# ScalarE's order in the scan loop, the scores around the scan input, and Gelu ahead of the last attention head

## The chip, the cores and the metric

The kernel runs on one core of a Trainium2 chip. The metric is the device time of one execution in microseconds, as the median over several runs. A core has TensorE (PE in the profile, with its weight loads as PEld), VectorE (DVE), ScalarE (ACT), GpSimd (POOL) and SyncE (SP, which issues most of the DMA transfers here). Each engine works through its own list of instructions in order, and waits on semaphores for what the others produce.

## The reference

Two layers over 256 tokens of width 1024. Each layer computes, in float32:

```
proj  = rms_norm(x) @ w_in            # q, k, v, u and two gate vectors
a     = differential attention: softmax(q0 k0) - lam * softmax(q1 k1), times v, 4 heads,
        then rms_norm per head
s     = bidirectional diagonal state-space scan of u (16 pairs of groups, both directions)
s     = gelu(s);  s = s * sigmoid(s @ w_glu)
x     = x + (g0 * (a @ w_branch0) + g1 * (s @ w_branch1)) @ w_out
x     = x + SwiGLU (layer 0)   or   top-2-of-8 expert SwiGLU (layer 1)
```

The change lies in the middle of the first five lines, once in each layer.

## The kernel before

Weights stream through SBUF in tiles of 128x2048 (1 MB). A tile is loaded into `raw` by SP, rounded by ScalarE into `hi` (`split` on ScalarE, L1016), and VectorE subtracts to get `lo` (`split` on VectorE, L1362). TensorE multiplies each tile as hi*hi, hi*lo and lo*hi, 24 matmuls of 512 columns (`proj`, printed as L549, since one helper issues nearly all matmuls). The tiles of a mixer are numbered from `t`; `t+8` to `t+15` belong to the gates, `t+16` is the second factor of the scan branch (`w_glu`), `t+17` to `t+20` the two branch matrices, `t+21` to `t+24` `w_out`.

The scan loop (`for s in range(8)`) handles in each turn three things at once: one of 8 attention blocks (head `s//2`, half of the tokens `s%2`), one of 8 pieces of the state-space scan, and one gate tile. What each engine does in turn `s`, in the order in which its code is written:

- TensorE: input of scan piece s+1 (`s5_in`, 32 small matmuls), the two halves of the scores of block s (`scores`, the second half waits for the first), transposes of the weights of block s-1 (`weights_t`, L704), the gate tile `t+8+s`, the attention output of block s-1 (`head_out`), and the scan output of piece s (`s5_out`). In the last turn `s5_out(7)` stands ahead of the gate tile.
- VectorE: `lo` of tile `t+10+s`, row minimum of block s (L1456), scan piece s+1 (`s5_scan`, L1429 to L1437), the softmax factors of block s (L1460, L1461), the combined weights of block s (L1468).
- ScalarE: tables for piece s+1 (`scan_tables`, L1121, L1127), `hi` of tile `t+10+s`, two exponentials of block s (L1071); in odd turns the evacuation of two gate banks through Tanh (`from_pj`, L1065); then `head_back` of block s-1, that is the copy of its transposed weights (L1083) for which `head_out` waits, and, once `head_out` is done, a copy (L1088) and a Square with a sum (L1089); and last the scaled second half of the softmax of block s (`scale_second`, L1077), for which VectorE's L1468 waits.
- GpSimd: the elementwise phase turns before and after each scan piece (`turn_forward`, L1893 to L1900); `s5_out` waits for them.

The scores of block s use the PSUM bank that VectorE's L1468 of block s-1 has read last, so `scores(s)` waits for it.

After the loop TensorE still has block 7: transposes, `head_out(7)`, then `channels`, 32 matmuls that regroup the scan's output after Gelu. ScalarE finishes block 7, takes the Sqrt for the heads' norm (L1194), runs Gelu (L1197), copies the regrouped scan output (L1200, `at_hi`), and VectorE makes its `lo` (L1558); then `proj(t+16)` can start. Between the halves of that projection TensorE transposes the attention output (`attention_t`, L567); after it, it transposes the scan output for the element-wise product (L567), and `proj(t+17)` follows, which needs the evacuation of `t+16` through Tanh (L1065 again) and both parts of the attention transposes (L1028 and L1376).

ScalarE evaluates functions from tables; `ACT_TABLE_LOAD` in the trace is a change of the loaded set.

Of the kernel before, what the change touches and what calls it, by code (L numbers as in the profile page):

```python
# [101 lines left out]
def build(nc, x, norm_mix, w_in, attn_lambda, attn_subln, ssm_lam_re, ssm_lam_im, ssm_log_dt, ssm_b_re, ssm_b_im,  # L102
# [6 lines left out]
    with ctx:  # L109
# [149 lines left out]
        def col(i, n=1):  # L259
            return small[:, i:i + n]  # L260
# [37 lines left out]
        def at_count(l, kind, g):  # L298
            return l * AT_PER_LAYER + AT_ORDER[(kind, g)] + 1
# [247 lines left out]
        def _(pe):  # L547
# [166 lines left out]
            def mixer(l):  # L714
# [54 lines left out]
                for s in range(8):  # L769
                    if s < 7:  # L770
                        s5_in(l, s + 1)
                    scores(l, s, 0)
                    scores(l, s, 1)
                    if s > 0:
                        weights_t(l, s - 1)
                    if s == 7:
                        s5_out(l, 7)
                    proj(t + 8 + s, l, 4 + s // 2, 4 * (s % 2), s % 2 == 0, s % 2 == 1)
                    if s == 0:
                        pe.wait_ge(pj_free[1], pj_read(l, 3))  # L780
                    if s > 0:
                        head_out(l, s - 1)
                    if s < 7:
                        s5_out(l, s)
                weights_t(l, 7)
                head_out(l, 7)
                channels(l)
# [12 lines left out]
                proj(t + 16, l, 8, 4, True, True, attention_t)  # L800
                pe.wait_ge(at_lo_ready, at_count(l, "a", 1))
                pe.wait_ge(s_ready, 2 * l + 2)
                for th in range(TH):
                    transposes((l, "s", th), [s_t[:, k, th * P:(th + 1) * P] for k in range(4)])
                proj(t + 17, l, 9, 0, True, True)
# [203 lines left out]
        def _(act):  # L1009
# [68 lines left out]

            def head_back(l, j):
                name = (l, "o", j)  # L1080
                bank = TR[TURN[name] % 2]
                act.wait_ge(wt_tr, 8 * l + j + 1)
                act.activation(wdiff_t, bank[:, 0:2 * P].rearrange("p (t q) -> p t q", t=2), ACT.Copy).then_inc(wt_ready, 1)  # L1083
                wait_turn(act, name)
# [45 lines left out]
            def mixer(l):  # L1130
# [48 lines left out]
                for s in range(8):  # L1179
# [3 lines left out]
                    probs_of(l, s)  # L1183
                    if s % 2 == 1:
                        i = 4 + s // 2
                        g, n = (i - 4) // 2, (i - 4) % 2
                        from_pj(l, i, t + 8 + s, lambda th: gates[:, th, g, n * 512:(n + 1) * 512], ACT.Tanh,
                                lambda th: col(RH + th))
                    if s > 0:
                        head_back(l, s - 1)  # L1190
                    scale_second(l, s)
                head_back(l, 7)
                act.wait_ge(avar_ready, l + 1)
                act.activation(col(AR, 8), col(AV, 8), ACT.Sqrt).then_inc(aroot_ready, 1)  # L1194
                act.wait_ge(y_done, DUOS * (l + 1))
                for half in range(2):
                    act.activation(s4[:, 512 * half:512 * half + 512], PY[half][:, :], ACT.Gelu).then_inc(gelu_ready, 1)  # L1197
                for th in range(TH):
                    act.wait_ge(chan_full, 2 * l + th + 1)
                    act.activation(at_hi[:, 4:8, th * P:(th + 1) * P], PV[th][:, :].rearrange("p (k s) -> p k s", k=4),  # L1200
                                   ACT.Copy).then_inc(at_hi_ready, 1)
                for th in range(TH):
# [153 lines left out]
        def _(dve):  # L1356
# [139 lines left out]
            def mixer(l):  # L1496
# [46 lines left out]

                wait_read(dve, (l, "o", 6))
# [4 lines left out]
                for th in range(TH):  # L1549
# [4 lines left out]
                    if th == 0:  # L1554
                        for h in range(TH):
                            half = slice(h * P, (h + 1) * P)
                            dve.wait_ge(at_hi_ready, at_count(l, "sa", h))
                            tt(at_lo[:, 4:8, half], PV[h][:, :].rearrange("p (k s) -> p k s", k=4),  # L1558
                               at_hi[:, 4:8, half].bitcast(f32), SUB).then_inc(at_lo_ready, 1)
# [418 lines left out]
```

## Time and profile before

| what | value |
|---|---|
| median of 3 runs | 1546.03 us (1545.55 to 1546.53) |
| the profiled execution | 1545.13 us, of which the span of the trace is 1543.3 us |
| busy: PE, PEld, DVE, ACT, POOL | 92%, 76%, 74%, 58%, 20% of the span |
| scan loop of layer 0 | about 129 to 209 us, its tail until 224 us |
| scan loop of layer 1 | about 558 to 639 us, its tail until 653 us |
| everything after the mixers | SwiGLU of layer 0 from 298 us, experts from 720 us |

The busy share of an engine says how much of the span it worked, not what bounds the end; for that the waits and the chain of work are read. All times in the rows below are microseconds from the start of the span.

### The profile page before, as it was taken

How to read it: one execution, taken by the hardware profiler on the slowest of the kernel's cores; microseconds unless marked ns; L12 is line 12 of the kernel's file. 1: busy time of each engine (PE TensorE's matmuls, PEld its weight loads, DVE VectorE, ACT ScalarE, POOL GpSimd, SP SyncE). 2: the span in 40 equal slices, each digit the busy share in tenths (PEclk: the TensorE clock that was granted, in tenths of full speed). 3: DMA queues.
4: the chain of work that ended last, by engine and by line, in shares of the span. 5: the costliest groups of instructions: out<-in, count | busy, mean ns of one | idle time of the engine just before them, and what ended most of it. 6: DMA issues, size and time to landing. Idle time of an engine off the chain costs nothing.

```text
span 1543.3 us, 24088 instructions
## 1 busy us (share of the span) xinstructions
PE 1423.8 (92%) x8701; PEld 1165.2 (76%) x8701; DVE 1146.9 (74%) x1125; ACT 894.3 (58%) x986; POOL 309.6 (20%) x354
## 2 busy tenths in 40 slices
PE   5688969999998989698999999999999999999995
PEld 3476748788887777487788888888878888888884
DVE  6966637655446556376888889888898899888985
ACT  4234544544335355444776777777677677676774
POOL 3747741998000067100000000000000000000000
PEclk9899979999999999898999999999999999999998
DMA  9332234555554423194999999999999999999970
GB/s 267 103 103 86 95 95 162 180 169 191 193 183 145 157 71 109 54 337 156 321 369 340 350 344 341 359 331 353 365 317 360 336 350 363 323 359 321 359 268 27
DMA packets 273808, 374.64 MB, mean 243 GB/s; under 512 B 17616, under 2 KB 220752, under 8 KB 273616
## 3 DMA queue, kind: packets, MB, share of 16 engines
q1 hardware_dynamic: 270176, 367.51, 70.8%
q0 software_dynamic: 1280, 3.15, 1.1%
q10 hardware_dynamic: 2288, 3.11, 0.6%
q8 instruction: 42, 0.69, 0.2%
q14 instruction: 22, 0.18, 0.0%
HBM read 371.63 MB, written 1.05 MB: 241 GB/s over the span
## 4 chain that ended last, share of the span: by engine, by line
PE 77%; DVE 8%; ACT 5%; issue 5%; DMA 1%; SPq 1%; POOL 1%; DVEq 0%; ACTq 0%; POOLq 0%
PE bank L549 75%; ACT hi L1016 3%; DVE lo L1362 3%; PE bank L946 1%; SPq L424 1%; PE bank L567 1%; DVE at_lo L1778 1%; DMA raw<-in_w_out_dram 1%; DMA areg<-in_norm_mix_dram 1%; DVE at_lo L1748 1%; DVE at_lo L1376 0%; PE bank L860 0%; PE bank L704 0%; POOL raw L1893 0%; ACT raw L1104 0%
## 5 line engine op out<-in xcount | busy, mean ns | idle before, releaser
L1362 DVE TENSOR_TENSOR lo<-raw,hi 128x2048 fp32r<-128x2048 f32 x347 | 805.2, 2325 | 191.4 <-ACT hi L1016 182.2
L1016 ACT ACTIVATE hi<-raw 128x2048 fp32r<-128x2048 f32 x347 | 662.9, 1914 | 115.0 <-PE bank L549 112.9
L549 PE MATMUL bank<-hi,at_hi 128*128 128x512 f32 x1280 | 518.3, 405 | 35.4 <-DVE areg L1414 13.7
L549 PE MATMUL bank<-hi,at_lo 128*128 128x512 f32 x1280 | 503.6, 393 | 0.0
L549 PE MATMUL bank<-lo,at_hi 128*128 128x512 f32 x1280 | 503.4, 393 | 0.0
L549 PEld LDWEIGHTS bank<-hi,at_hi 128*128 128x128 f32 x1280 | 242.9, 190 | 89.7 <-issue 17.3
L549 PEld LDWEIGHTS bank<-hi,at_lo 128*128 128x128 f32 x1280 | 242.8, 190 | 52.2
L549 PEld LDWEIGHTS bank<-lo,at_hi 128*128 128x128 f32 x1280 | 243.7, 190 | 46.1
L549 PE MATMUL bank<-hi,ht_hi 128*128 128x512 f32 x440 | 172.2, 391 | 4.4 <-DVE ht_lo L1679 3.5
L549 PE MATMUL bank<-hi,ht_lo 128*128 128x512 f32 x440 | 171.3, 389 | 0.0
L549 PE MATMUL bank<-lo,ht_hi 128*128 128x512 f32 x440 | 171.3, 389 | 0.0
L1272 ACT ACTIVATE ht_hi<-bank 128x256 fp32r<-128x256 f32 (+1 forms) x99 | 40.5, 409 | 167.2 <-PE bank L946 122.3
L549 PEld LDWEIGHTS bank<-hi,ht_hi 128*128 128x128 f32 x440 | 82.6, 188 | 24.7 <-DVE ht_lo L1679 6.1
L549 PEld LDWEIGHTS bank<-hi,ht_lo 128*128 128x128 f32 x440 | 82.6, 188 | 17.3
L549 PEld LDWEIGHTS bank<-lo,ht_hi 128*128 128x128 f32 x440 | 82.6, 188 | 16.9
L1893 POOL TENSOR_TENSOR raw<-raw 128x256 f32<-128x256 f32 x64 | 48.4, 787 | 217.8 <-issue 188.1
L1679 DVE TENSOR_TENSOR ht_lo<-bank,ht_hi 128x256 fp32r<-128x256 f32 (+1 forms) x99 | 44.3, 448 | 42.4 <-ACT ht_hi L1272 42.4
L549 PE MATMUL bank<-raw 64*64 64x64 f32 (+1 forms) x1664 | 51.8, 235 | 14.7 <-issue 8.6
L1310 ACT ACTIVATE vreg<-bank 128x256 f32<-128x256 f32 x88 | 33.8, 384 | 53.0 <-PE bank L549 53.0
L549 PEld LDWEIGHTS bank<-raw 64*64 64x64 f32 (+1 forms) x1664 | 48.3, 135 | 18.4 <-issue 9.8
L549 PE MATMUL bank<-vreg,qk 128*128 128x128 f32 x320 | 42.4, 285 | 10.8 <-ACT qk L1083 9.4
L549 PEld LDWEIGHTS bank<-vreg,qk 128*128 128x128 f32 x320 | 40.2, 198 | 15.8 <-ACT qk L1083 13.2
(265 smaller groups left out, 1096.5 us busy)
## 6 DMA issues: line engine op xcount, KB each, us to landing
raw<-in_moe_w_dram SPq DMA_DIRECT2D x528, 512.0 KB, 5.5
raw<-in_ffn_w_dram SPq DMA_DIRECT2D x66, 512.0 KB, 4.2
raw<-in_w_in_dram SPq DMA_DIRECT2D x64, 512.0 KB, 4.6
raw<-in_w_branch_dram SPq DMA_DIRECT2D x16, 512.0 KB, 4.1
raw<-in_w_out_dram SPq DMA_DIRECT2D x16, 512.0 KB, 4.9
raw<-in_w_glu_dram SPq DMA_DIRECT2D x4, 512.0 KB, 4.2
xres<-in_x_dram SPq DMA_DIRECT2D x2, 512.0 KB, 6.1
areg<-in_norm_mix_dram ACTq DMA_DIRECT2D x2, 512.0 KB, 6.4
```

The source lines that it names most:

```text
L424: sp.dma_start(dst, src).then_inc(raw_full[slot], 16)
L549: return pe.matmul(o, a, b, start=start, stop=stop)
L567: last = pe.transpose(bank[:, i * rows:(i + 1) * rows], src, ident[0:rows, 0:rows])
L946: m = pe.transpose(TR[0][:, f * P:(f + 1) * P], v_flat[:, FC + f * P:FC + (f + 1) * P], ident)
L1016: act.activation(hi[:, slot, :], src, ACT.Copy).then_inc(hi_ready, 1)
L1272: act.activation(ht_hi[:, :, 0:cols], TR[0][:, 0:2 * cols].rearrange("p (f s) -> p f s", f=2), ACT.Copy).then_inc(ht_hi_ready, 1)
L1310: act.activation(v_flat[:, 0:FC], h_bank(c)[:, 0:FC], ACT.Silu).then_inc(g_ready, 1)
L1362: tt(lo[:, slot, :], src, hi[:, slot, :].bitcast(f32), SUB).then_inc(lo_ready, 1)
L1679: tt(ht_lo[:, :, 0:cols], TR[0][:, 0:2 * cols].rearrange("p (f s) -> p f s", f=2), ht_hi[:, :, 0:cols].bitcast(f32), SUB).then_inc(ht_lo_r ...
L1748: tt(at_lo[:, 4 * g:4 * g + 4, 0:P], banks[4 + g][:, :].rearrange("p (k c) -> p k c", k=4), at_hi[:, 4 * g:4 * g + 4, 0:P].bitcast(f32), S ...
L1778: m = stt(at_lo[:, 4 * n:4 * n + 4, P:2 * P], PY[n][:, :].rearrange("p (k c) -> p k c", k=4), place_gate, at_hi[:, 4 * n:4 * n + 4, P:2 * ...
L1893: last = tt(dst, src[:, :, :, d, :], w[:, r:r + 1, :, d, :].broadcast_to([P, 2, 2, 64]), MUL)
```

## The change

On ScalarE the copy of the transposed weights is taken out of `head_back` (`weights_back`) and stands right behind the exponentials, `scale_second` follows it, then come the gates of the odd turns, then the rest of `head_back`. In the last turn Gelu stands between `scale_second` and the gates. After the loop the copies of the regrouped scan output stand ahead of the rest of block 7 and of the Sqrt.

On TensorE the first half of the scores stands ahead of `s5_in`, `channels` ahead of `head_out(7)`, and the attention transposes stand behind `proj(t+16)` instead of between its halves. VectorE makes the `lo` of the regrouped scan output ahead of the heads' norm.

```diff
                 for s in range(8):
+                    scores(l, s, 0)
                     if s < 7:
                         s5_in(l, s + 1)
-                    scores(l, s, 0)
                     scores(l, s, 1)
...
                 weights_t(l, 7)
+                channels(l)
                 head_out(l, 7)
-                channels(l)
                 pe.wait_ge(at_lo_ready, at_count(l, "sa", 1))
...
-                proj(t + 16, l, 8, 4, True, True, attention_t)
+                proj(t + 16, l, 8, 4, True, True)
+                attention_t()
+                pe.wait_ge(s_ready, 2 * l + 2)
+                for th in range(TH):
+                    transposes((l, "s", th), [s_t[:, k, th * P:(th + 1) * P] for k in range(4)])
                 pe.wait_ge(at_lo_ready, at_count(l, "a", 1))
-                pe.wait_ge(s_ready, 2 * l + 2)
-                for th in range(TH):
-                    transposes((l, "s", th), [s_t[:, k, th * P:(th + 1) * P] for k in range(4)])
                 proj(t + 17, l, 9, 0, True, True)
...
+            def weights_back(l, j):
+
+                act.wait_ge(wt_tr, 8 * l + j + 1)
+                act.activation(wdiff_t, TR[TURN[(l, "o", j)] % 2][:, 0:2 * P].rearrange("p (t q) -> p t q", t=2),
+                               ACT.Copy).then_inc(wt_ready, 1)
...
                     probs_of(l, s)
+                    if s > 0:
+                        weights_back(l, s - 1)
+                    scale_second(l, s)
+                    if s == 7:
+                        act.wait_ge(y_done, DUOS * (l + 1))
+                        for half in range(2):
+                            act.activation(s4[:, 512 * half:512 * half + 512], PY[half][:, :], ACT.Gelu).then_inc(gelu_ready, 1)
...
                     if s > 0:
                         head_back(l, s - 1)
-                    scale_second(l, s)
+                weights_back(l, 7)
+                for th in range(TH):
+                    act.wait_ge(chan_full, 2 * l + th + 1)
+                    act.activation(at_hi[:, 4:8, th * P:(th + 1) * P], PV[th][:, :].rearrange("p (k s) -> p k s", k=4),
+                                   ACT.Copy).then_inc(at_hi_ready, 1)
                 head_back(l, 7)
```

What the instruction lists show. In the first place, an odd turn of the loop on ScalarE (turn 1 of layer 0), bank6 holds the scores, bank7 the transposed weights and the attention output, bank0 and bank1 the gate tiles. Before:

```order
L1071 ACTIVATE bank6,small<-bank6,small 128x256
L1065 ACTIVATE gates<-bank0,small 128x512 [waits pj0_full]
L1065 ACTIVATE gates<-bank1,small 128x512 [waits tile_used]
L1083 ACTIVATE qk<-bank7 128x256 [waits wt_tr]
L1088 ACTIVATE areg<-bank7 128x128 [waits cbm_in,tr_full]
L1089 ACTIVATE bank7,small<-bank7 128x128 [waits act_own]
L1077 ACTIVATE qk<-bank6,small 128x256 [waits factor_ready]
L1121 ACTIVATE raw<-par 128x4x63 [waits zs_ready]
L1127 ACTIVATE raw<-raw 128x4x32 [waits wtab_half]
L1127 ACTIVATE raw<-raw 128x4x32
L1016 ACTIVATE hi<-raw 128x2048 [waits tile_used,raw_full0]
```

The same turn with the change (its line numbers stand 1 to 8 higher):

```order
L1072 ACTIVATE bank6,small<-bank6,small 128x256
L1083 ACTIVATE qk<-bank7 128x256 [waits wt_tr]
L1078 ACTIVATE qk<-bank6,small 128x256 [waits factor_ready]
L1066 ACTIVATE gates<-bank0,small 128x512 [waits pj0_full]
L1066 ACTIVATE gates<-bank1,small 128x512 [waits tile_used]
L1092 ACTIVATE areg<-bank7 128x128 [waits cbm_in,tr_full]
L1093 ACTIVATE bank7,small<-bank7 128x128 [waits act_own]
L1125 ACTIVATE raw<-par 128x4x63 [waits zs_ready]
L1131 ACTIVATE raw<-raw 128x4x32 [waits wtab_half]
L1131 ACTIVATE raw<-raw 128x4x32
L1017 ACTIVATE hi<-raw 128x2048 [waits tile_used,raw_full0]
```

The gates and the two instructions of `head_back` stood ahead of the scaled second half (L1077) and now stand between it (L1078) and the next tile's `hi` (L1017).

In the second place, ScalarE after the loop in layer 0. Before:

```order
L1194 ACT_TABLE_LOAD
L1194 ACTIVATE small<-small 128x8 [waits avar_ready]
L1197 ACT_TABLE_LOAD
L1197 ACTIVATE raw<-bank 128x512 [waits y_done]
L1197 ACTIVATE raw<-bank 128x512
L1200 ACTIVATE at_hi<-bank 128x4x128 [waits chan_full] x2
L1204 ACTIVATE ureg<-bank 128x4x128 [waits at_lo_ready] x2
L1016 ACTIVATE hi<-raw 128x2048 [waits tile_used,raw_full0]
L1028 ACTIVATE at_hi<-bank 128x4x128 [waits tr_full] x2
L1050 DMA areg<-in_norm_ffn_dram 128x1024
L1065 ACTIVATE qk<-bank 128x512 [waits pj0_full]
L1065 ACTIVATE qk<-bank 128x512 [waits tile_used]
```

With the change, from the copies of the regrouped scan output on (Gelu and its table load stand in the last turn of the loop now):

```order
L1205 ACTIVATE at_hi<-bank 128x4x128 [waits chan_full] x2
L1092 ACTIVATE areg<-bank 128x128 [waits tr_full]
L1093 ACTIVATE bank,small<-bank 128x128 [waits act_own]
L1209 ACT_TABLE_LOAD
L1209 ACTIVATE small<-small 128x8 [waits avar_ready]
L1212 ACTIVATE ureg<-bank 128x4x128 [waits at_lo_ready] x2
L1017 ACTIVATE hi<-raw 128x2048 [waits tile_used,raw_full0]
L1029 ACTIVATE at_hi<-bank 128x4x128 [waits tr_full] x2
L1051 DMA areg<-in_norm_ffn_dram 128x1024
L1066 ACT_TABLE_LOAD
L1066 ACTIVATE qk<-bank 128x512 [waits pj0_full]
L1066 ACTIVATE qk<-bank 128x512 [waits tile_used]
```

The Sqrt is now behind Gelu, and a third table load per layer stands ahead of the Tanh that evacuates tile `t+16`.

In the third place, TensorE after the last gate tile of layer 0. L704 are the transposes of block 7, `qk` with `vreg` is `head_out`, `raw` with `cst` is `channels`. Before:

```order
L549 MATMUL bank<-vreg,qk 128x128 [waits wt_ready]
L549 MATMUL bank<-vreg,qk 128x128
L704 MATMUL bank<-cst,qk 128x128 [waits w_ready]
L704 MATMUL bank<-cst,qk 128x128
L549 MATMUL bank<-vreg,qk 128x128 [waits wt_ready]
L549 MATMUL bank<-vreg,qk 128x128
L549 MATMUL bank<-raw,cst 32x4x64 [waits gelu_ready]
L549 MATMUL bank<-raw,cst 32x4x64 x15
L549 MATMUL bank<-hi,at_hi 128x512 [waits pj_free0,lo_ready,at_lo_ready]
```

With the change:

```order
L549 MATMUL bank<-vreg,qk 128x128 [waits wt_ready]
L549 MATMUL bank<-vreg,qk 128x128
L704 MATMUL bank<-cst,qk 128x128 [waits w_ready]
L704 MATMUL bank<-cst,qk 128x128
L549 MATMUL bank<-raw,cst 32x4x64 [waits gelu_ready]
L549 MATMUL bank<-raw,cst 32x4x64 x15
L549 MATMUL bank<-vreg,qk 128x128 [waits wt_ready]
L549 MATMUL bank<-vreg,qk 128x128
L549 MATMUL bank<-hi,at_hi 128x512 [waits pj_free0,lo_ready,at_lo_ready]
```

`head_out(7)` moved from before `channels` to behind it.

## Rows read from the trace of the kernel before

**Rows 1.** Grouped waits of TensorE, 133 to 228 us: total us, times, longest.

```profile
PE bank L549 <- ACT qk L1083: 4.7, 5, 1.1
```

**Rows 2.** Timeline of ScalarE, loop of layer 0: start, length, what, [idle before, releaser].

```profile
153.63 1.91 ACT L1016 ACTIVATE hi<-raw 128x2048 fp32r<-128x2048 f32 x1
...
161.46 0.69 ACT L1065 ACTIVATE gates<-bank,small 128x512 f32<-128x512 f32 x1 [1.14 <-PE bank L549]
162.05 0.38 ACT L1083 ACTIVATE qk<-bank 128x256 f32<-128x256 f32 x1
163.23 0.28 ACT L1088 ACTIVATE areg<-bank 128x128 f32<-128x128 f32 x1 [0.80 <-PE bank L549]
...
163.80 0.47 ACT L1077 ACTIVATE qk<-bank,small 128x256 f32<-128x256 f32 x1
164.16 0.41 ACT L1121 ACTIVATE raw<-par 128x252 f32<-128x252 f32 x1
...
164.86 1.90 ACT L1016 ACTIVATE hi<-raw 128x2048 fp32r<-128x2048 f32 x1
...
186.01 1.90 ACT L1016 ACTIVATE hi<-raw 128x2048 fp32r<-128x2048 f32 x1
```

**Rows 3.** Timeline of VectorE, loop of layer 0: three factor instructions and one split.

```profile
140.85 0.16 DVE L1461 TENSOR_TENSOR small<-small 128x1 f32<-128x1 f32 x1
...
162.33 0.16 DVE L1461 TENSOR_TENSOR small<-small 128x1 f32<-128x1 f32 x1
...
173.42 0.16 DVE L1461 TENSOR_TENSOR small<-small 128x1 f32<-128x1 f32 x1
...
197.14 2.32 DVE L1362 TENSOR_TENSOR lo<-raw,hi 128x2048 fp32r<-128x2048 f32 x1 [1.31 <-ACT hi L1016]
```

**Rows 4.** Timeline of GpSimd, the last two instructions of the last scan piece.

```profile
197.39 2.65 POOL L1899 TENSOR_TENSOR raw<-raw 128x256 f32<-128x256 f32 x1
200.00 0.72 POOL L1900 TENSOR_TENSOR raw<-raw 128x256 f32<-128x256 f32 x1
```

**Rows 5.** Chain of work that ended last, 183 to 234 us: start, length, what.

```profile
200.77 8.51 PE bank L549 x64
...
212.77 0.43 PE bank L704 x2
...
213.66 0.73 PE bank L549 x4
...
215.10 1.28 ACT L1194
...
224.13 4.78 PE bank L549 x12
...
229.78 2.75 PE bank L549 x12
```

**Rows 6.** Timeline of ScalarE, the second copy of the attention transposes, layer 0.

```profile
229.88 0.59 ACT L1028 ACTIVATE at_hi<-bank 128x512 fp32r<-128x512 f32 x1
```

**Rows 7.** Timeline of TensorE, first matmul of projection t+17, layer 0.

```profile
233.17 0.48 PE L549 MATMUL bank<-hi,at_hi 128*128 128x512 f32 x1
```

**Rows 8.** Chain of work, layer 1: the gates behind the last gate tile.

```profile
638.76 0.69 ACT gates L1065
```

**Rows 9.** Timeline of TensorE, layer 1: channels, first matmuls of t+16 and t+17.

```profile
648.50 3.23 PE L549 MATMUL bank<-raw,cst 128*32 128x256 f32 x32 [4.68 <-ACT raw L1197]
...
653.19 0.50 PE L549 MATMUL bank<-hi,at_hi 128*128 128x512 f32 x1 [1.45 <-DVE at_lo L1558]
...
660.47 0.48 PE L549 MATMUL bank<-hi,at_hi 128*128 128x512 f32 x1
```

**Rows 10.** Timeline of VectorE, layer 1: `lo` of tile t+18.

```profile
655.60 2.29 DVE L1362 TENSOR_TENSOR lo<-raw,hi 128x2048 fp32r<-128x2048 f32 x1 [1.42 <-ACT hi L1016]
```

**Rows 11.** Busy time by window: us, PE, PEld, DVE, ACT, POOL, granted clock, DMA, GB/s.

```profile
141.00:162.00 21.00, 19.98 (x212) 15.86 (x212) 13.91 (x21) 10.73 (x29) 17.05 (x24) 1.00 0.30 94
...
200.00:210.00 10.00, 8.49 (x64) 6.98 (x64) 0.38 (x3) 2.41 (x7) 7.24 (x11) 0.83 0.54 146
```

More of the change, by code:

```diff
@@ L799, in gated_s_t @@
                         transposes((l, "s2", th), heads_of(s_gated, th))
-                proj(t + 16, l, 8, 4, True, True, attention_t)
-                pe.wait_ge(at_lo_ready, at_count(l, "a", 1))
+                proj(t + 16, l, 8, 4, True, True)
+                attention_t()
                 pe.wait_ge(s_ready, 2 * l + 2)
@@ L804, in mixer @@
                     transposes((l, "s", th), [s_t[:, k, th * P:(th + 1) * P] for k in range(4)])
+                pe.wait_ge(at_lo_ready, at_count(l, "a", 1))
                 proj(t + 17, l, 9, 0, True, True)
@@ L1077, in scale_second @@
                 act.activation(second, TR[TURN[(l, "sc", j)] % 2][:, SEQ:2 * SEQ], ACT.Copy, scale=col(C1)).then_inc(second_scaled, 1)
+            def weights_back(l, j):
+                act.wait_ge(wt_tr, 8 * l + j + 1)
+                act.activation(wdiff_t, TR[TURN[(l, "o", j)] % 2][:, 0:2 * P].rearrange("p (t q) -> p t q", t=2),
+                               ACT.Copy).then_inc(wt_ready, 1)
             def head_back(l, j):
                 name = (l, "o", j)
[L1081 to L1084, printed above, removed]
+                bank = wait_turn(act, name)
                 h, th = j // 2, j % 2
@@ L1190, in mixer @@
                         head_back(l, s - 1)
-                    scale_second(l, s)
[L1192 to L1197, printed above, removed]
+                weights_back(l, 7)
                 for th in range(TH):
@@ L1201, in mixer @@
                                    ACT.Copy).then_inc(at_hi_ready, 1)
+                head_back(l, 7)
+                act.wait_ge(avar_ready, l + 1)
+                act.activation(col(AR, 8), col(AV, 8), ACT.Sqrt).then_inc(aroot_ready, 1)
                 for th in range(TH):
@@ L1542, in mixer @@
                     weights(l, s)
+                for h in range(TH):
+                    half = slice(h * P, (h + 1) * P)
+                    dve.wait_ge(at_hi_ready, at_count(l, "sa", h))
+                    tt(at_lo[:, 4:8, half], PV[h][:, :].rearrange("p (k s) -> p k s", k=4),
+                       at_hi[:, 4:8, half].bitcast(f32), SUB).then_inc(at_lo_ready, 1)
                 wait_read(dve, (l, "o", 6))
@@ L1553, in mixer @@
                     m.then_inc(a_ready, 1)
[L1554 to L1559, printed above, removed]
                 split_static(t + 18)
```

## The prediction

> **What bounds the kernel now.** I read four views, in this order. The grouped waits of TensorE show who stops it in the loop: in layer 0 it waits five times, 4.7 us in all, for the copy of the transposed weights (L1083) [rows 1], which stands on ScalarE behind the second gate bank and so behind the end of the gate tile. Between these waits TensorE is busy (19.98 of 21.00 us in the window of turns 1 to 3) and the clock is at 2.4 GHz [rows 11]. The loop is TensorE's, then, but the timelines of ScalarE and VectorE show a second loop close behind, and it is the one the change touches. The chain of waits shows the tail: from the end of the last gate tile (200.77 + 8.51 = 209.28) to the first matmul of `t+16` (224.13) it takes 14.85 us, through six hand-overs and two table loads of 1.28 us in a row [rows 5], with TensorE all but idle. Layer 1 repeats this: 638.76 to 653.19, 14.43 us [rows 8, 9]. What comes after is a steady stream on TensorE, so I take a shift there one to one into the end.
>
> **The second loop.** VectorE makes `lo`, the row minimum, the next scan piece and the factors in one go; it starts when ScalarE's `hi` is there. From the start of `hi` to the end of the factors: 153.63 to 162.49, and 164.86 to 173.58, 8.86 and 8.72 us, mean 8.79 [rows 2, 3]. Then ScalarE runs `scale_second`, 163.80 to 164.16 (0.36), the tables, 164.16 to 164.86 (0.70), and the next `hi` [rows 2]. Before the change nothing else stands between factors and `hi`, if the rest was done under the scan.
>
> **What the loop costs after the change.** The rest of `head_back`, 163.23 to 163.80 (0.57), and in odd turns the two Tanh, 2 x 0.59 = 1.18 (161.46 to 162.05 is one pitch), now stand between factors and the next `hi` [rows 2]. With 0.04 for a hand-over (POOL's end 200.72 to TensorE's 200.77 [rows 4, 5]) an even turn's tail is 0.04 + 0.36 + 0.57 + 0.70 = 1.67 and an odd one's 2.85. Two turns take 2 x 8.79 + 4.52 = 22.10 us; before they took 164.86 to 186.01, 21.15 [rows 2]. So the order that frees TensorE from its wait of up to 1.1 in each odd turn [rows 1] makes ScalarE and VectorE the bound, 0.95 slower per pair. From the first factors (141.01 [rows 3]), which nothing moves, to the `hi` of turn 6 there are three odd and two even tails and four stretches: 141.01 + 8.55 + 3.34 + 35.16 = 188.06 instead of 186.01, **+2.05**. The scan piece of turn 6 and GpSimd's states for `s5_out(7)`, for which TensorE waits at 200.77, are late by that. Scores ahead of `s5_in` hide the first half's drain, but TensorE, with 21.15 - 1.1 = 20.05 us of work in 22.10, waits for `weights` anyway: counted at nothing. If this cover were gone, it would gain at most a few tenths per turn.
>
> The bounds of this term: GpSimd's L1899 began 0.25 after VectorE's split and took 2.65, until 0.6 behind the split's end (199.46), where its neighbour L1900 took 0.72 [rows 3, 4]. Which of the two meets the split depends on the phase. If it is L1900 alone, the states come with the split's end and one instruction behind it, 199.46 + 0.7 and so 0.6 less late; if both are held, one instruction more, +0.6.
>
> **The tail.** Scaling, weights and Gelu of the last turn now run under the last gate tile: Gelu needs `s5_out(7)`, which ends where the 5.5 us of the gate tile begin, then 1.28 for its table and, as an estimate from the two 512-column Tanh, 1.2 for itself: it is done 3 us before the gate tile. What is left behind the gate tile on TensorE is `head_out(6)` 0.73 (as the one at 213.66), the transposes of block 7 0.43 [rows 5], `channels` 3.23, and from its end (651.73) to `t+16` (653.19) 1.46 for `at_hi` and `at_lo` [rows 9]. `head_out(7)` fits into these 1.46. Sum 5.85. So `t+16` starts at 209.28 + 2.05 + 5.85 = 217.18 in layer 0, 6.95 earlier, and at 638.76 + 2.05 + 5.85 = 646.66 in layer 1, 6.53 earlier.
>
> **From t+16 to t+17.** Before this took 233.17 - 224.13 = 9.04 in layer 0, where the first half ran at a low clock (4.78 for 12 matmuls against 2.75 [rows 5]), and 7.28 in layer 1 [rows 7, 9]. After: 24 matmuls, 2 x 2.75 and 0.1 for filling, 5.6. The attention transposes follow, and their second copy starts 0.97 behind the matmuls (228.91 to 229.88 [rows 5, 6]), at 6.6; the next ScalarE instruction comes 0.5 later, and it is now a table load, 1.28 (as the Sqrt's at 215.10), then Tanh 0.6: 9.0 us after the start the bank is free and `t+17` can begin. The other path into `t+17` is shorter: `hi` of `t+18` behind Sqrt and two copies, its `lo` 2.29 [rows 10] done at about 6.85, then two `at_lo` of 0.65, 8.15. What the halves of `t+16` used to hide, the trip of the attention transposes over ScalarE and VectorE, is thus open now, 9.0 - 5.6 - 1.7 for both sets of transposes, 1.7 us. Layer 0: 217.18 + 9.0 = 226.2 against 233.17, **-7.0**. Layer 1: 655.7 against 660.47, -4.8. In layer 1 the `w_out` loads, queued among expert tiles, are let go by `lo` of `t+18`: before 657.89 - 653.19 = 4.7 after the start of `t+16`, now 6.85, so this stream moves by 6.53 - 2.15 = 4.4 only [rows 9, 10]. I take **-4.6** between the two.
>
> At the table load the Trainium skill speaks against the change. The row has the load at 1.28 us and the chain has nothing behind it: the Sqrt's load begins where block 7's Square ends [rows 5]. "ScalarE: Activation LUTs", section "What ACT_TABLE_LOAD costs", gives 1.283 us for the load and 1.38 us more for a drain at each change of set; by that the estimate would be 1.4 us more per layer, -8.8 in all. By the row it is -11.6.
>
> **Sum.** -7.0 - 4.6 = -11.6. The profiled execution took 1545.13 (span 1543.3 and 1.8 around it), so 1533.5; the median of before is 0.9 higher, **1534.4 us**. A measurement of this kernel tells about 0.2%, 3.1 us, from no change.
>
> **Rivals.**
> - *The loop loses nothing.* If the second loop has slack that I don't see, both +2.05 fall away: -15.7, 1530.3. For it: TensorE did set the pace before. Against: every stretch of 8.79 is serial on two in-order engines. Chance 0.13.
> - *The table load costs twice.* A pause as long as the load itself, behind the third load of each layer, delays `t+17` by 1.3 each: 1537.0. For it: the load stands alone on the way to `t+17`. Against: no such pause in the chain. The skill's drain, above, would be this case. Chance 0.11.
> - *Layer 1's gain is held by its loads.* If the 10 MB of `w_out` and expert tiles arrive when they did before, the 4.6 are lost: 1539.0. For it: the stream of loads is dense there. Against: its trigger moves by 4.4. Chance 0.12.
> - *Slower: the clock.* TensorE's idle time per pair of turns grows from 1.1 to over 2. In the window behind the wait for `s5_out(7)` the granted share was 0.83; in the loop with its waits of 1.1 it was 1.00 [rows 1, 11]. If the longer gaps bring 1.2 GHz into the loop, a gate tile takes 4.78 x 2 instead of 5.5, some 4 us more, and a turn then is TensorE's at about 14 us instead of 11: 3 us in each of 12 turns, 36 us, 1570. It decides from the fourth such turn on. "TensorE: Matmul & The Clock Gate", section "HAM oscillation — how this bites in real kernels", has such an oscillation from regular waits in a loop; the window of the loop with waits of 1.1 does not show it. Against: the gaps stay under 2 us. Chance 0.05.
> - *It gives nothing to speak of*, a new wait in the tail that eats most of it, as Gelu late for `channels`: it would have to come some 14 us later than I sum in the two layers together, since it has 4 us of cover in each (3 and the 1.16 ahead of `channels`). Near 1546. Chance 0.04.
>
> My case has 0.55. Its own range is 1532 to 1537 (GpSimd's collision, -0.6 to +0.6 per layer, and either path into `t+17`, 8.15 or 9.0). The range for 8 in 10 takes in the loop without loss and the held loads: 1529.5 to 1539.5. Faster by over 0.2%: my case, the first three rivals, less a little for two of them together with a slower loop, 0.89; within 0.2%: 0.05; slower 0.06.
>
> **What the profile after would show.** In odd turns no wait of TensorE for the weights' copy; instead a wait for VectorE's combined weights ahead of `scores(s)` of about 0.8 and 1.9 us in alternating turns. `hi` tiles 22.1 us apart per pair, and the wait ahead of `s5_out(7)` ending at 202.8. No table load between the end of the last gate tile and `t+16`, and 5.9 us between them. A table load and about 1.7 us of idle TensorE ahead of `t+17`. `t+16` at 217.2, and in layer 1 at 639.7 (646.66 less the 7.0 of layer 0). Wrong would be: a `hi` pace of 21.1 or less (first rival), a granted clock below 1 in the loop (the fourth), ScalarE idle for loads in layer 1 between `t+20` and `t+24` (the third).

## The result and the profile after

The changed kernel takes 1534.28 us (median of 4 runs, 1533.64 to 1534.79), the one before 1545.79 us beside it (4 runs, 1545.37 to 1546.53): a ratio of 0.9925, 95% interval 0.9908 to 0.9942. The profiled execution took 1534.32 us with a span of 1532.5. The forecast was 1534.4.

The sum came out, but several of its terms did not; they cancel in part. So the stages are read one at a time. First the grouped waits of TensorE of the changed kernel, 133 to 228 us, where [rows 1] had the copy of the transposed weights:

```profile
PE bank L549 <- DVE qk L1476: 4.3, 4, 1.5
PE bank L549 <- POOL raw L1907: 3.3, 1, 3.3
PE bank L567 <- DVE at_lo L1384: 1.1, 1, 1.1
PE bank L549 <- DVE at_lo L1555: 0.8, 1, 0.8
```

The waits for the copy are gone. Of the 4.7 us in [rows 1] three waits of 1.05 us lay in the loop; the other two stood in its tail (TensorE before):

```profile
210.32 0.71 PE L549 MATMUL bank<-vreg,qk 128*128 128x128 f32 x4 [1.05 <-ACT qk L1083]
...
213.66 0.71 PE L549 MATMUL bank<-vreg,qk 128*128 128x128 f32 x4 [0.47 <-ACT qk L1083]
```

In place of the 3.1 us in the loop TensorE now waits 4.3 us there for the combined weights (L1476) ahead of the scores: the loop's wait has moved and grown, it has not gone.

Timeline of ScalarE in the loop of layer 0, which answers to [rows 2]:

```profile
142.69 0.47 ACT L1078 ACTIVATE qk<-bank,small 128x256 f32<-128x256 f32 x1 [2.52 <-DVE small L1469]
143.06 0.68 ACT L1066 ACTIVATE gates<-bank,small 128x512 f32<-128x512 f32 x1
145.32 0.69 ACT L1066 ACTIVATE gates<-bank,small 128x512 f32<-128x512 f32 x1 [1.57 <-PE bank L549]
...
147.17 1.90 ACT L1017 ACTIVATE hi<-raw 128x2048 fp32r<-128x2048 f32 x1
...
169.36 1.90 ACT L1017 ACTIVATE hi<-raw 128x2048 fp32r<-128x2048 f32 x1
...
191.55 1.90 ACT L1017 ACTIVATE hi<-raw 128x2048 fp32r<-128x2048 f32 x1
```

The `hi` tiles are 22.19 us apart per pair of turns (169.36 to 191.55) where they were 21.15 [rows 2]. The first odd turn shows something more: between the two Tanh ScalarE waits 1.57 us for TensorE's gate tile, and the next `hi` stands behind that wait, as it did in the old order.

VectorE and GpSimd at the end of the loop, as in [rows 3, 4]:

```profile
142.50 0.16 DVE L1469 TENSOR_TENSOR small<-small 128x1 f32<-128x1 f32 x1
...
203.10 2.70 DVE L1370 TENSOR_TENSOR lo<-raw,hi 128x2048 fp32r<-128x2048 f32 x1 [1.88 <-ACT hi L1017]
```

```profile
202.94 0.72 POOL L1906 TENSOR_TENSOR raw<-raw 128x256 f32<-128x256 f32 x1
203.62 2.77 POOL L1907 TENSOR_TENSOR raw<-raw 128x256 f32<-128x256 f32 x1
```

One of GpSimd's two last instructions is held again while VectorE's split runs, the other of them than before; from the start of the first to the end of the second it is 3.4 us before (197.39 to 200.72) and 3.5 now. The first factors meant in the prediction, those of turn 1, end at 142.66 here and at 141.01 before. This 1.65 us does not come from the moved instructions: the `hi` of turn 0 already starts at 120.51 instead of 118.85, and the distance stays the same up to here. The point differs from run to run (138.12 to 142.66 over all kernels below), so I count the stages from it.

TensorE from the last scan output on, answering to [rows 5, 7, 9]:

```profile
201.28 1.45 PE L549 MATMUL bank<-qk,ureg 64*128 64x256 f32 x4 [1.45 <-DVE qk L1476]
...
206.44 2.40 PE L549 MATMUL bank<-raw 64*64 64x64 f32 x40 [3.29 <-POOL raw L1907]
...
214.77 0.60 PE L549 MATMUL bank<-vreg,qk 128*128 128x128 f32 x4
215.21 0.38 PE L704 MATMUL bank<-cst,qk 128*128 128x128 f32 x2
215.53 1.93 PE L549 MATMUL bank<-raw,cst 128*32 128x256 f32 x32
...
218.90 0.50 PE L549 MATMUL bank<-hi,at_hi 128*128 128x512 f32 x1 [0.80 <-DVE at_lo L1555]
...
224.48 1.04 PE L567 MATMUL bank<-cst,areg 128*128 128x128 f32 x8
226.59 1.16 PE L567 MATMUL bank<-cst,ureg 128*128 128x128 f32 x8 [1.07 <-DVE at_lo L1384]
228.26 0.47 PE L549 MATMUL bank<-hi,at_hi 128*128 128x512 f32 x1 [0.51 <-ACT qk L1066]
```

No table load lies on the way from the gate tile (its end is 206.44 + 8.51 = 214.95, the same 8.51 as in [rows 5]) to `t+16` (the Sqrt's starts at 218.83, when `t+16` is ready), and the way is 3.95 us instead of 14.85. `channels` take 1.93 us; they took 3.23 in [rows 9].

Against the point where the first factors end, in layer 0:

| from the first factors to | before | after | difference |
|---|---|---|---|
| `hi` of turn 6 | 45.00 | 48.89 | +3.89 |
| `s5_out(7)` | 59.76 | 63.78 | +4.02 |
| `t+16` | 83.12 | 76.24 | -6.88 |
| `t+17` | 92.16 | 85.60 | -6.56 |

Layer 1 from `t+17` of layer 0 to its own: 427.30 before [rows 7, 9]; after, by TensorE's timeline there:

```profile
637.21 1.93 PE L549 MATMUL bank<-raw,cst 128*32 128x256 f32 x32
...
640.58 0.50 PE L549 MATMUL bank<-hi,at_hi 128*128 128x512 f32 x1 [0.80 <-DVE at_lo L1555]
...
649.95 0.47 PE L549 MATMUL bank<-hi,at_hi 128*128 128x512 f32 x1 [0.51 <-ACT qk L1066]
```

649.95 - 228.26 = 421.69, so -5.61. From there to the end the span changes by -0.28 (882.83 to 882.55). With the +1.65 ahead of the factors: 1.65 - 6.56 - 5.61 - 0.28 = -10.8, the difference of the two spans.

### The profile page after: what moved, and what is told of

Same layout as the page of the kernel before. It is cut to its first block, busy times and chain, and to the rows that moved or that the text cites. A ratio compares the mean times of both kernels' runs of the same rounds, so it can differ in the third digit from the quotient of the medians.

```text
span 1532.5 us, 24090 instructions
## 1 busy us (share of the span) xinstructions
PE 1423.9 (93%) x8701; PEld 1166.7 (76%) x8701; DVE 1148.6 (75%) x1125; ACT 896.0 (58%) x988; POOL 309.7 (20%) x354
## 3 DMA queue, kind: packets, MB, share of 16 engines
HBM read 371.63 MB, written 1.05 MB: 243 GB/s over the span
## 4 chain that ended last, share of the span: by engine, by line
PE 72%; DVE 11%; ACT 7%; issue 6%; DMA 1%; SPq 1%; POOL 1%; ACTq 0%; DVEq 0%; POOLq 0%
PE bank L549 70%; ACT hi L1017 4%; DVE lo L1370 3%; SPq L424 1%; PE bank L947 1%; DVE raw L1445 1%; PE bank L567 1%; DVE at_lo L1785 1%; DMA areg<-in_norm_mix_dram 1%; DMA raw<-in_w_out_dram 1%; DVE at_lo L1755 1%; DVE bank L1438 0%; DVE small L1464 0%; DVE raw L1437 0%; POOL raw L1907 0%
## 5 line engine op out<-in xcount | busy, mean ns | idle before, releaser
L1017 ACT ACTIVATE hi<-raw 128x2048 fp32r<-128x2048 f32 x347 | 663.0, 1914 | 116.2 <-PE bank L549 113.5
L1072 ACT ACTIVATE bank<-bank,small 128x256 f32<-128x256 f32 x32 | 14.2, 443 | 53.0 <-DVE small L1464 53.0
```

The source lines that it names most:

```text
L1017: act.activation(hi[:, slot, :], src, ACT.Copy).then_inc(hi_ready, 1)
```

## The experiments

Eleven runs of eight kernels in three groups, each group beside runs of the kernel before; the first group ran on one chip, the other two on another. Times compare directly only inside a group.

### First group: the parts of the loop

`e1_noswap`: the change without its first edit on TensorE.

```diff
-                    scores(l, s, 0)
                     if s < 7:
                         s5_in(l, s + 1)
+                    scores(l, s, 0)
                     scores(l, s, 1)
```

> The changed kernel with one part undone: the scan input (32 small matmuls) stands ahead of both score halves again. Theory S: the alternation of scores and scan input keeps TensorE's clock at 1.2 GHz for longer behind the first stall of the loop (granted 0.50 from 133 to 139 us, where the kernel before had 0.97), so without it turn 1 comes about 1.7 us earlier in each layer: 1531, about 3 us less than the changed kernel's 1534.3. Rival: the low clock has another cause, and the order of scores is worth nothing either way: 1534.3 within 0.5.

`e2_scale_last`: that, and in turns 0 to 6 the scaled second half last, with the copy of the weights still first.

```diff
                     if s > 0:
                         weights_back(l, s - 1)
-                    scale_second(l, s)
                     if s == 7:
+                        scale_second(l, s)
...
                     if s > 0:
                         head_back(l, s - 1)
+                    if s < 7:
+                        scale_second(l, s)
```

> As the run without the alternation, and in turns 0 to 6 the scaled second half stands last on ScalarE again, behind gates and the rest of block s-1; only the copy of the transposed weights stays ahead of the gates; turn 7 and the tail as changed. Theory M (the serial loop of ScalarE and VectorE sets the pace after the change, because gates and the rest of block s-1 stand between the factors and the next tile's hi): the hi tiles come 20.1 us apart per pair instead of 22.2, the last scan piece about 7 us earlier in each layer, 1520. Rival F (that loop is free and TensorE sets the pace): at most 1 us less than the run without the alternation.

`e3_old_loop`: `e1_noswap` with turns 0 to 6 of ScalarE wholly in the old order (gates, copy, rest of `head_back`, scaled second half); turn 7 and everything behind it as in the change.

> The changed kernel with turns 0 to 6 of the scan loop wholly as before (ScalarE: gates, weights copy, rest of block s-1, scaled second half; scan input ahead of the scores); turn 7 and everything behind it as changed. Theory M: the loop costs what it cost before, 3.9 us per layer less than after the change, and the tail keeps its gain: 1526.5. Rival F: 1534 or more, since the 1.05 us waits of odd turns come back (3 per layer), up to 1540.

`e4_loop_only`: the kernel before with nothing but the new order on ScalarE in the loop; Gelu, `channels` and the copies behind the loop stay where they were.

> The kernel before with only ScalarE's order in the scan loop changed (transposed weights, second half, then gates and the rest), TensorE's order and the tail as before. Theory M: each layer loses 2 us in the loop's pace, and gains 2.4 to 2.7 behind the last gate tile, where the attention output and the transposes of block 7 no longer wait for ScalarE: within 1 us of the kernel before, 1545 to 1546.5; if the longer low clock belongs to this order too, 1.7 more per layer, 1549. Rival F: about 5 us less than before for the waits removed and the shorter end, 1538 to 1541.

Measured, the kernel before at 1544.54 us (13 runs):

| kernel | us | ratio, 95% | `hi` per pair | factors to `s5_out(7)` | `s5_out(7)` to `t+16` |
|---|---|---|---|---|---|
| `e1_noswap` | 1529.13 | 0.9905 (0.9882 to 0.9927) | 22.2 | 62.2 | 12.96 |
| `e3_old_loop` | 1523.26 | 0.9875 (0.9846 to 0.9903) | 21.2 | 61.5 | 12.38 |
| `e2_scale_last` | 1519.73 | 0.9846 (0.9823 to 0.9869) | 20.1 | 57.0 | 13.74 |
| `e4_loop_only` | 1544.78 | 1.0001 (0.9987 to 1.0014) | 22.2 | 63.4 | 21.57 |

The stages are those of layer 0. `e1_noswap` came out below the 1531 us of the theory of the scores, which seemed to bear it out, but no run of the change itself stood beside it; the second group has that comparison. `e2_scale_last` met its 1520 us. `e3_old_loop` was forecast at 1526.5 us and came out at 1523.26.

ScalarE's timeline of `e2_scale_last`, a pair of turns, the end of the factors on VectorE, and TensorE's grouped waits in its loop and tail (133 to 215 us):

```profile
151.83 1.90 ACT L1017 ACTIVATE hi<-raw 128x2048 fp32r<-128x2048 f32 x1
...
160.81 0.47 ACT L1078 ACTIVATE qk<-bank,small 128x256 f32<-128x256 f32 x1 [0.42 <-DVE small L1471]
...
171.93 1.90 ACT L1017 ACTIVATE hi<-raw 128x2048 fp32r<-128x2048 f32 x1
```

```profile
160.62 0.16 DVE L1471 TENSOR_TENSOR small<-small 128x1 f32<-128x1 f32 x1
```

```profile
PE bank L549 <- POOL raw L1909: 3.2, 1, 3.2
PE bank L549 <- DVE qk L1478: 1.0, 1, 1.0
PE bank L549 <- DVE at_lo L1557: 0.8, 1, 0.8
```

The chain over ScalarE and VectorE still sets the pace: from `hi` (151.83) to the end of the factors (160.78) it takes 8.95 us and from there to the next `hi` (161.89) 1.11, 10.06 for a turn, and ScalarE idles 0.42 us for the factors ahead of the scaled half. TensorE has next to no room left: a pair takes 20.10 us, and its own work was worked out to be 20.05. The same waits of `e3_old_loop`:

```profile
PE bank L549 <- ACT qk L1083: 3.1, 3, 1.1
PE bank L549 <- POOL raw L1910: 3.0, 1, 3.0
...
PE bank L549 <- DVE qk L1479: 0.3, 1, 0.3
```

With the old order the old wait is back, and the kernel is 5.9 us faster than with the new one, though the two intervals overlap by a hair (0.9882 and 0.9903). By the traces it is 1.25 us faster in layer 0 and 4.29 in layer 1, where 2.05 in each was expected; in layer 0 its turn 1 had part of the gate tile at the lower clock (granted 0.74 from 132 to 138 us), and the next `hi` came 4.42 us behind the first factors, against 2.83 in `e1_noswap`. So the old order does not guard against a late gate tile either. The 13.74 us of `e2_scale_last` have their reason on TensorE: `s5_out(7)` and the last gate tile together take 9.8 us (13.74 less the 3.95 behind them) instead of the 8.51 of the change, since more of the gate tile's matmuls ran at the lower clock (granted 0.50 from 197 to 201 us). That belongs to the execution rather than to the order: the same stretch took 9.8 us in `f1_after_again` too. In `e4_loop_only`, where the tail of before is kept but for the earlier scaled half, the slower loop takes all that the earlier half gives back (23.36 to 21.57 us from `s5_out(7)` to `t+16`): no difference in time, as forecast. So the new order on ScalarE by itself costs the loop about 1 us per pair, and the whole gain of the change comes from the tail.

### Second group: the scores, the table load, the attention transposes

`f1_after_again` is the change as it is, `f2_noswap_again` the kernel of `e1_noswap`.

> The changed kernel once more, on the chip of the next three, as their base. Theory S (alternating scores and scan input keep the clock low for longer at the start of the loop): again 6 us or more at 1.2 GHz behind the loop's first stall in both layers, and 3 us more than the same kernel without the alternation. Rival P (how long the clock stays low there differs from run to run and from kernel to kernel, whatever the order of the scores: the runs without the alternation had 0, 3.4, 6.8 and 10.3 us of it): another length than the first time, and no more than 1 us between the two.

> The changed kernel with the scan input ahead of both score halves, once more, beside the changed kernel on one chip. Theory S: 3 us less than the changed kernel (0.2%). Rival P: within 1 us of it in the median, apart from an even spread.

`f3_no_table_load` evacuates `t+16` by a plain copy, so that no table is loaded there; it leaves out the sigmoid of the scan branch's gate.

```diff
-                from_pj(l, 8, t + 16, lambda th: s_gated[:, th, :], ACT.Tanh, scale=0.5)
+                from_pj(l, 8, t + 16, lambda th: s_gated[:, th, :], ACT.Copy, scale=0.5)
```

> The changed kernel with Copy in place of Tanh at the evacuation of tile t+16 (the sigmoid of the scan branch is left out there), so that the third table load of each layer is gone. Theory T (the load of 1.28 us costs what is not covered by the other path into t+17, the lo of the attention transposes, which ends 0.5 us earlier): 0.5 us less per layer, the wait of 0.51 us ahead of t+17 gone and that of 1.07 us ahead of the scan transposes unchanged, 1 us less in all. Rival D (load and a drain behind it, 2.66 us): 1.9 us less or more.

`f4_between` puts the attention transposes back between the halves of `t+16`.

```diff
-                proj(t + 16, l, 8, 4, True, True)
-                attention_t()
+                proj(t + 16, l, 8, 4, True, True, attention_t)
```

> The changed kernel with the attention transposes between the halves of projection t+16 again. Theory: the attention rows are ready 3.9 us behind the start of t+16, the first half ends at 2.8, so 1.1 us of idle TensorE stands in the middle, but the trip over ScalarE and VectorE lies under the second half; t+17 starts at 8.5 instead of 9.4 us behind t+16: 0.85 us less per layer, 1.7 in all. Rival: the projection is cut later and the trip ends no sooner, so nothing within 0.5 us.

Measured, the kernel before at 1546.69 us (11 runs):

| kernel | us | ratio, 95% | `t+16` to `t+17`, layer 0 and 1 |
|---|---|---|---|
| `f1_after_again` | 1530.33 | 0.9904 (0.9888 to 0.9921) | 9.38 and 9.40 |
| `f2_noswap_again` | 1530.83 | 0.9907 (0.9888 to 0.9926) | 9.37 and 9.36 |
| `f3_no_table_load` | 1532.83 | 0.9919 (0.9900 to 0.9937) | 8.60 and 8.62 |
| `f4_between` | 1528.98 | 0.9893 (0.9875 to 0.9911) | 8.43 and 8.45 |

The order of the scores makes no difference that can be measured: the medians are 0.5 us apart, and the runs of either kernel spread over 4 to 5 us. The theory that it kept TensorE at the lower clock at the start of the loop is not borne out: the windows of 6 us at 126 and 132 us show granted clocks of 0.54 and 0.61 with it, 0.50 and 0.67 without it, and the `hi` of turn 2 came 4.08 and 4.07 us behind the factors of turn 1. A small share of the order is not excluded. In layer 0 this distance was longer than usual by over 1 us in all five profiled executions with the first scores ahead, and in four of the eight without; in layer 1 in one of the five and in two of the eight.

TensorE of `f3_no_table_load`, and then of `f4_between`:

```profile
215.65 0.50 PE L549 MATMUL bank<-hi,at_hi 128*128 128x512 f32 x1 [0.80 <-DVE at_lo L1555]
...
223.34 1.16 PE L567 MATMUL bank<-cst,ureg 128*128 128x128 f32 x8 [1.07 <-DVE at_lo L1384]
224.25 0.48 PE L549 MATMUL bank<-hi,at_hi 128*128 128x512 f32 x1
```

```profile
214.60 0.50 PE L549 MATMUL bank<-hi,at_hi 128*128 128x512 f32 x1 [0.80 <-DVE at_lo L1554]
...
218.55 1.09 PE L567 MATMUL bank<-cst,areg 128*128 128x128 f32 x8 [0.92 <-DVE areg L1564]
...
223.03 0.48 PE L549 MATMUL bank<-hi,at_hi 128*128 128x512 f32 x1
```

Without the table load the wait of 0.51 ahead of `t+17` is gone and the 1.07 ahead of the scan transposes stays: the load costs 0.78 us, not its 1.28, since the transposes then set the start. With the attention transposes between the halves their trip over ScalarE and VectorE is hidden again, the table load too, and TensorE pays 0.92 for the heads' norm instead. That is 0.95 us less in each layer by the traces, where 0.85 was expected. In the medians neither difference can be told apart from zero.

`f3_no_table_load`, forecast at 1 us less than the change, is 2.5 us slower by the medians, and its trace shows a part of that: behind one of the regular waits of the loop the clock fell, in both layers. TensorE, and the window (columns as below):

```profile
174.97 0.70 PE L549 MATMUL bank<-qk,ureg 64*128 64x256 f32 x2 [1.45 <-DVE qk L1476]
175.59 1.84 PE L549 MATMUL bank<-raw 64*64 64x64 f32 x32
```

```profile
175.00:182.00 7.00, 7.00 (x46) 5.22 (x47) 4.47 (x4) 3.63 (x9) 6.84 (x10) 0.56 0.10 27
```

The same 32 matmuls take 1.15 us at 2.4 GHz (168.24 us in the changed kernel), and the `hi` tiles around this stretch are 12.66 us apart instead of 11.9, in layer 0 (175.56 to 188.22) and in layer 1 alike: about 0.8 us lost per layer, as much as the missing load gives back. In layer 0 the edit lies behind this stretch, so it is not what made the clock fall there.

### Third group: the two gains together

`g1_best` joins the edits of `e2_scale_last` and `f4_between`; the other two are repeated beside it.

> The scaled second half last, and the attention transposes between the halves of t+16 again. Theory M (each part is paid where the instruction lists say, and the two lie in different stages, so they add): the loop as in the kernel with the scaled second half last, hi 20.1 us apart per pair of turns; t+16 to t+17 8.4 instead of 9.4 us, no wait of TensorE for at_lo ahead of t+17. Against that kernel on the same chip 2 x 0.9 = 1.8 us less in the profile's two stages, ratio to before about 0.9835. Rival W (the time won between t+16 and t+17 comes back as waits for loads later): the same median as that kernel within 0.5 us, with longer waits for the w_out tiles in layer 1.

> The kernel with the scaled second half last once more, on another chip and with more rounds, as the yardstick. Theory M: ratio to before 0.9845 plus or minus 0.0015, 9 to 10 us below the change as it is in the same call; hi 20.1 us apart per pair. Rival (its gain over the change came from a clock that happened to stay at 2.4 GHz in that execution): ratio 0.990, like the change.

> The change as it is, beside the two others on one chip. Theory M: ratio 0.990 to 0.992; hi 22.2 us apart per pair of turns, waits of TensorE for the combined weights (L1476) of about 4 us in the loop of layer 0, t+16 to t+17 9.4 us. Rival as for the kernel with the scaled second half last: all three within 0.2%.

Measured, the kernel before at 1545.39 us (9 runs): `g1_best` 1518.28 us, ratio 0.9810 (0.9793 to 0.9827); `g2_scale_last_again` 1519.07, 0.9830 (0.9817 to 0.9844); `g3_after_third` 1533.70, 0.9917 (0.9903 to 0.9931). The scaled half last is worth 14.6 us against the change by the medians (12.3 by the two spans), where 9 to 10 were expected; its interval lies well below that of `g3_after_third`. Its ratio lies on the lower bound of what was expected (0.9845 less 0.0015), and that of `g1_best` 0.0025 below its 0.9835. `g1_best` starts `t+17` 8.43 us after `t+16` in layer 0, as `f4_between` did. The last wait of ScalarE for a `w_out` tile in layer 1, of `g1_best` and then of `g2_scale_last_again`:

```profile
666.22 1.92 ACT L1016 ACTIVATE hi<-raw 128x2048 fp32r<-128x2048 f32 x1 [1.27 <-DMA raw<-in_w_out_dram]
```

```profile
667.72 1.92 ACT L1017 ACTIVATE hi<-raw 128x2048 fp32r<-128x2048 f32 x1 [1.52 <-DMA raw<-in_w_out_dram]
```

They end 31.4 us behind the `t+17` of layer 1 (634.80) in the one and 31.7 us (636.06) in the other, so the longer wait for loads that the rival asked for is not there. The median of `g1_best` is 0.8 us below `g2_scale_last_again` with overlapping intervals, where 1.8 was summed. The sum of the two gains fits, but the medians do not tell it from a smaller one; that stays open.

## Why the prediction came out right

**The loop: right in kind, too small.** The first half of the term holds: the odd turns' waits went, the bound became ScalarE and VectorE, and a pair takes 22.19 us where the sum gave 22.10. `e2_scale_last` shows that this is the mechanism: with the scaled half last a pair takes 20.1 us, and `e3_old_loop` has the 21.2 of before. The step that was mis-sized in layer 0 is "an even turn's tail is 0.04 + 0.36 + 0.57 + 0.70 = 1.67 and an odd one's 2.85", which takes the gate bank as full when ScalarE comes to it. In turn 1 it was not: TensorE ran the first part of the gate tile at the lower clock. Windows of the changed kernel around it (us, PE, PEld, DVE, ACT, POOL, granted clock, DMA, GB/s):

```profile
127.00:133.00 6.00, 1.92 (x38) 1.95 (x40) 4.66 (x10) 1.79 (x6) 5.84 (x12) 0.85 0.52 175
133.00:139.00 6.00, 6.00 (x48) 4.27 (x46) 3.27 (x3) 2.43 (x4) 5.92 (x7) 0.50 0.00 0
139.00:145.00 6.00, 6.00 (x23) 4.78 (x22) 3.97 (x9) 2.23 (x7) 5.29 (x11) 0.79 0.55 179
147.00:200.00 53.00, 49.97 (x532) 40.11 (x530) 35.27 (x53) 24.88 (x64) 32.09 (x48) 1.00 0.30 99
```

TensorE is mostly idle in the first window, at 1.2 GHz in the second and partly in the third, and at 2.4 GHz through the rest of the loop. So 1.66 of the 3.89 us are this wait, 0.18 the pace, and 2.05 what was forecast. The 1.66 are no cost of the new order: `e3_old_loop`, with the old one, paid for a late gate tile in the same turn too (4.42 us), and in layer 1 the changed kernel did not (2.97). Counted from the factors of turn 1 to `s5_out(7)`, the loop lost 4.02 us in layer 0, outside the 0.6 either way that the term allowed, and 2.49 in layer 1 (59.98 to 62.47), inside it. `e1_noswap`, whose turn 1 had no such wait, came to 47.27 us from the factors to the `hi` of turn 6, against 47.05 by the sum. Why the lower clock lasts longer in one execution than in another was not found.

**The tail: right in kind, too dear by 1.9 us.** `t+16` starts 3.95 us after the gate tile, not 5.85. The step that failed is "`channels` 3.23": the row was read as the work of 32 matmuls, but it stands behind 4.68 us of idle time [rows 9], and the windows around it in the trace of before have a granted clock of 0.50 in layer 0 and 0.60 in layer 1 (columns as above):

```profile
215.00:222.00 7.00, 2.95 (x28) 1.36 (x32) 1.83 (x7) 4.54 (x7) 0.00 (x0) 0.50 0.19 40
648.00:652.00 4.00, 3.23 (x32) 1.37 (x32) 0.69 (x1) 1.23 (x3) 0.00 (x0) 0.60 0.00 0
```

Behind the gate tile without a gap they take 1.93 us at a granted clock of 1.00. In `e4_loop_only`, which keeps the idle 4.68, they take 3.32 and 3.64. That is 1.3 of the 1.9 us. The other 0.6 lie in `head_out(6)` and the transposes, 0.58 us from the end of the gate tile (214.95) to `channels` (215.53), where I had taken 0.73 + 0.43 from [rows 5], which stand behind waits too. From the end of `channels` (217.46) to `t+16` it is 1.44, as the 1.46 of the sum. So this is a gain that the change did bring and that the sum left out; in layer 0 it happens to be as large as what the loop cost beyond the forecast.

**t+16 to t+17: 9.36 and 9.37 us instead of 9.0.** The path named, over the third table load, does come last. Left out was the wait of the scan transposes (1.07) for the evacuation of the attention transposes; since it lies mostly under the same load, it is no extra term. The idle time ahead of `t+17`, 1.07 + 0.51, is near the 1.7 forecast. ScalarE's timeline there:

```profile
226.23 1.28 ACT L1066 ACT_TABLE_LOAD   x1
227.52 1.08 ACT L1066 ACTIVATE qk<-bank 128x512 f32<-128x512 f32 x2
```

The Tanh starts 0.01 us behind the load, so the rival in which the load costs twice is out. The Trainium skill, "ScalarE: Activation LUTs", section "What ACT_TABLE_LOAD costs", has 1.283 us for the load and a drain of 1.38 us more. This trace bears out the first (1.28) and does not show the second; the measurement decides.

**Layer 1 and its loads.** -5.61 us at `t+17` where -4.8 was summed: counted from the `t+17` of layer 0, `s5_out(7)` lost 1.89 us (of the 2.49 above 0.6 were won ahead of the loop), the tail was as short as in layer 0, the gate tile 0.9 us longer, and `t+16` to `t+17` 0.4 longer than summed. The loads moved with their trigger: the last wait of ScalarE for a `w_out` tile ends at 681.99 instead of 691.78, 9.8 us earlier for a `t+17` that is 10.5 earlier. Before and after:

```profile
691.78 1.92 ACT L1016 ACTIVATE hi<-raw 128x2048 fp32r<-128x2048 f32 x1 [1.21 <-DMA raw<-in_w_out_dram]
```

```profile
681.99 1.92 ACT L1017 ACTIVATE hi<-raw 128x2048 fp32r<-128x2048 f32 x1 [1.89 <-DMA raw<-in_w_out_dram]
```

So at that point 0.7 us is given back to the loads, where the sum had the stream move 0.4 us less than `t+17`. None of it reaches the end: from `t+17` on the kernel is 0.28 us shorter than before. The rival in which the loads hold everything is out.

**The swap counted at nothing** made no difference that the runs could measure (`f1_after_again` against `f2_noswap_again`, 0.5 us apart).

**The clock falls in the loop: out at the price forecast, but not as a mechanism.** In the profiled execution the longer waits, 0.71 and 1.45 us in alternating turns (0.8 and 1.9 forecast), left the granted clock at 1.00 from 147 to 200 us. They did not in every execution of this loop: in `f3_no_table_load` the clock fell behind a wait of 1.45 us once in each layer, for some 7 us and about 0.8 us of time, and in `f1_after_again`, the change itself, it fell behind the last such wait of layer 0 (granted 0.76 from 196 to 200 us). That is far from the 36 us of the rival. "TensorE: Matmul & The Clock Gate", section "HAM oscillation — how this bites in real kernels" of the Trainium skill, was named for this rival, for an oscillation from regular waits in a loop. The clock of `f3_no_table_load` was back at 1.00 from 183 to 190 us and did not fall again until the longer wait for `s5_out(7)`, so no run here shows an oscillation with waits of this length.

**The first rival, a loop that loses nothing,** is out by the pace of 22.19. That the total was met to 0.1 us is in good part luck: in layer 0 +2.0 in the loop and -1.9 in the tail cancel, in layer 1 the -1.9 meet +0.9 in the gate tile and +0.4 behind it, and the profiled execution lost 1.65 us ahead of all that was moved.

## What to carry to other kernels

On an engine that works in order, an urgent instruction can be moved forward only by moving others back: ask for each of these whose next start it delays. Here the copy that TensorE waited for had to come first, but the scaled half, moved up with it, pushed the gates and the rest of `head_back` in front of the next tile's `hi`. Leaving it last gives both, 1519 instead of 1534 us. A short group of matmuls behind several us of idle time is priced at the lower clock; when the change takes the idle time away, price it again.

## What the runs showed of the hardware

- The same 32 matmuls (`channels`) took 3.64 and 3.23 us behind 4.68 us of idle time in the kernel before, at granted clocks of 0.50 and 0.60, and 1.93 us at 1.00 without it.
- At the start of the loop TensorE is at 1.2 GHz for a stretch that differs between executions: windows of 6 us at 132 and 138 us show 0.74 and 1.00 in `e3_old_loop`, 1.00 and 1.00 in `e2_scale_last`, and in the changed kernel 0.50 and 0.71.
- With waits of 0.70 and 1.45 us in alternating turns the granted clock stayed at 1.00 from 147 to 200 us in the changed kernel, and in `f3_no_table_load`, with the same loop, fell to 0.56 (window of 7 us at 175 us) behind a wait of 1.45.
- The changes of table cost 1.28 us each and nothing behind them: the Tanh starts 0.01 us behind its load. Taking the third load of a layer away gave 0.78 us, since another wait set the start then.
- An elementwise instruction of GpSimd on 128x256 took 2.65 and 2.77 us where it began behind VectorE's split of 128x2048 and beside it, and 0.72 us where it began after the split's end or 0.16 us ahead of the split.
